# A layer with routed experts: filled TensorE waits, an earlier weight load, and shared work on the last routed rows

## The chip, the core and the metric

The kernel runs on one core of a Trainium2 chip. The core has five engines with a queue each: TensorE (PE, matrix products), VectorE (DVE), ScalarE (ACT), GpSimd (POOL) and SyncE (SP), which here only asks for transfers. 16 DMA engines carry the transfers. The metric is the device time of one execution in microseconds, as the median of the runs.

## The reference

One layer is computed for 128 prompt tokens and 512 sample tokens, five tiles of 128 rows, with a width of 1024. After norm, retention and differential attention, three projections lead to the residual `x1`. Then comes the part that matters here:

```python
h2 = rmsnorm(x, n2) * (1.0 + sc2) + sh2
x = x + g2 * hier_moe(h2, ...)          # and a last rmsnorm

# hier_moe: 4 groups of 8 experts, best group, best 2 experts in it
p_grp = softmax(hf @ rgw + rgb)
p_top, g_idx = top_k(p_grp, 1)
e_logits = (hf @ rew + reb).reshape(-1, 4, 8)     # those of the group
e_top, e_idx = top_k(softmax(e_logits), 2)
w = p_top * e_top / sum(e_top)
a = silu(hf @ wg[e]) * (hf @ wu[e])               # 256 wide
y = (a * w) @ wd[e]
```

Each of the 32 experts has 1 MB each of gate, up and down weights in fp32. All are read.

## The kernel before, in words

Every engine has its own program, written out by hand; semaphores tie them together. A list `plan`, which all engines walk, sets the order up to the last projection `wo1`; what follows it is written out one after the other for each engine.

**Rows and logits.** The tiles go in the order `ORDER = (4, 0, 1, 2, 3)`; tile 4 is the prompt. For a sample tile, VectorE multiplies `x1` by a scale row (`scaled_input`, plan item `M`), GpSimd forms the root of the mean square (`inverse_root`), and VectorE multiplies by the root and adds a shift row (`router_input`, plan item `N`): that is the tile `h2[t]`. It is stored to DRAM (`h2_dram`): the three middle tiles by SP (`row_store`, semaphore `st_h2_mid`), the last, tile 3, by ACT (`st_h2_ends`). TensorE forms the logits from `x1` without waiting for the root, 36 a token; VectorE scales them afterwards by the root, five small instructions, one for each tile, once the last root and the last rows are there.

**Routing.** VectorE picks group and experts in some 25 small instructions. TensorE counts ranks (L1328 to L1335, semaphore `pe_rank`), VectorE turns them into places, and TensorE's `places` (L1342) builds tables of which token stands in which place of an expert's block of 64: first rows (`idx_ready`), then choices, then weights.

**Experts.** Experts are worked in 16 pairs. For each pair GpSimd asks for an indirect transfer that gathers 128 token rows into `xg` (L2476, semaphores `ld_xg`), TensorE transposes them (`gathered`, L1359), ACT copies them out of PSUM, and TensorE multiplies with gate and up weights (L1366, in the first pair L1373 in two halves, semaphores `pe_gate0` and `pe_gu`), then with down weights (L1386, `pe_dn`). VectorE gates the rows, and GpSimd asks for the scattering transfer. At the end the rows of both experts are added and normalised.

**Weights.** SP asks for all weights, in the order of its program. There are six buffers for gate and up weights and six for down weights, three pairs' worth. Those of pairs 0 to 2 are asked for around `wo1` and behind it; those of pair 3 and later only when TensorE has finished with the buffer (`pe_gate0`, `pe_gu`, `pe_dn`). Between the two stands this stretch of SP's program (L925 to L936):

```python
load_gate_or_up(1, 3, 3); load_gate_up(2, 2)
for x in ld_xg: sp.wait_ge(x, 16)        # both gathers have landed
sp.wait_ge(x1_ready, 2 * NT); sp.wait_ge(st_h2_mid, 16 * 3)
load_down(4, 4)
sp.wait_ge(h2_ready, PT)
load_gate_or_up(1, 4, 4)
...                                      # two modulation rows, 0.5 MB each
```

`load_down(e, slot)` asks for an expert's down weights, `load_gate_or_up(g, e, slot)` for the gate (g = 0) or up (g = 1) weights. An instruction of SP that waits holds all behind it.

Of the kernel before, what the change touches and what calls it, by code (L numbers as in the profile page):

```python
# [27 lines left out]
ALU = mybir.AluOpType  # L28
# [3 lines left out]
P = 128  # L32
D = 1024
KC = D // P
HK = KC // 2
NT = 5
# [76 lines left out]
def build(nc, a, o, coff, roff, nconst, nroute):  # L113
    ctx = ExitStack()
    with ctx:  # L115
        sem_names = {}

        def sem(name):
            s = ctx.enter_context(nc.semaphore(name))
            sem_names[name] = s  # L120
            return s
# [529 lines left out]
        scale_made = sem("scale_made")  # L651
        prompt_scaled = sem("prompt_scaled")
# [35 lines left out]
        def _(sp):  # L688
# [149 lines left out]
            def load_down(e, slot):  # L838
                sp.dma_start(w_dn[slot], a["moe_w_down"][0, e].rearrange("(p k) n -> p k n", p=P)).then_inc(ld_dn[slot], 16)
# [86 lines left out]
            for x in ld_xg:  # L926
                sp.wait_ge(x, 16)
            sp.wait_ge(x1_ready, 2 * NT)
            sp.wait_ge(st_h2_mid, 16 * 3)
            load_down(4, 4)  # L930
            sp.wait_ge(h2_ready, PT)
            load_gate_or_up(1, 4, 4)
# [65 lines left out]
        def _(pe):  # L998
# [324 lines left out]

            pe.wait_ge(route_a, 1)
# [21 lines left out]
            halves = lambda v: v.rearrange("p (n i) -> p i n", i=2)  # L1346
            pe.wait_ge(route_a, 3)
# [3 lines left out]
            places(B(6), hot_rank, lambda x, i: halves(hot_row[:, x, 2, :])[:, i, :], PAIRS)  # L1351
            pe.wait_ge(route_d, 6)
# [68 lines left out]

            pe.wait_ge(idx_ready, 1)
            pe.wait_ge(ld_xg[0], 16)
            gathered(0).then_inc(pe_xt, 1)
            for p in range(PAIRS - 1):
                pair(p, p % 2, 2 * (p % 3), p // 2, p // 3, first=(p == 0))
# [64 lines left out]
        def _(act):  # L1491
# [236 lines left out]
            act.wait_ge(h2_ready, PT)  # L1728
            act.dma_start(h2_dram[3 * P:PT * P, :], h2[3]).then_inc(st_h2_ends, 16)
# [74 lines left out]
        def _(dve):  # L1804
            chain = [0]

            def link(ins):
                chain[0] += 1
                ins.then_inc(dve_chain, 1)
                dve.wait_ge(dve_chain, chain[0])  # L1810
# [226 lines left out]
            def router_input(t):  # L2037

                q = place_of[t]
                if q == 0:  # L2040
                    dve.wait_ge(ld_route, 16 * 6)
                    dve.wait_ge(ld_row2, 16 * 4)
                    for i in (1, 0):
                        dve.scalar_tensor_tensor(out=scale2[i], in0=scale2[i], scalar=1.0, in1=n2_row,
                                                 op0=ALU.add, op1=ALU.mult).then_inc(scale_made, 1)
                    dve.wait_ge(scale_made, 2)
                    return
                dve.wait_ge(roots, q + 1)
                dve.scalar_tensor_tensor(out=h2[t], in0=h2[t], scalar=rstd[:, t:t + 1], in1=shift2[0],
                                         op0=ALU.mult, op1=ALU.add).then_inc(h2_ready, 1)  # L2050
                if q < PT:
                    return

                dve.wait_ge(pe_logits, NT)
                for u in ORDER:
                    ins = dve.scalar_tensor_tensor(out=logits[:, u, :], in0=logit_out(u), scalar=rstd[:, u:u + 1],
                                                   in1=logit_bias[:, 1 if u == PT else 0, :], op0=ALU.mult, op1=ALU.add)
                link(ins)

            def scaled_input(t):  # L2060

                dve.wait_ge(x1_ready, x1_done[t])
                if t == 3:
                    dve.wait_ge(st_h2_ends, 16)
                link(dve.tensor_tensor(h2[t], x1[:, t, :], scale2[0], ALU.mult))
# [326 lines left out]
        def _(pool):  # L2392
# [74 lines left out]

            pool.wait_ge(idx_ready, 1)
# [16 lines left out]
            rows_in(1)  # L2485
            pool.wait_ge(idx_ready, 2)
# [56 lines left out]
```

## Time and profile before

| | us |
|---|---|
| median of 3 runs (lowest to highest) | 1154.61 (1154.06 to 1155.63) |
| the profiled execution | 1152.95 |
| its span | 1151.1 |

| engine | busy us | share of the span |
|---|---|---|
| TensorE | 1063.4 | 92% |
| VectorE | 580.1 | 50% |
| ScalarE | 404.4 | 35% |
| GpSimd | 101.2 | 9% |

The busy shares are means over stages with different limits. The page also cuts the span into 40 equal slices and gives for each the busy tenths, the granted clock of TensorE (9 is 90% or more of 2.4 GHz), the busy share of the DMA engines and the gigabytes a second they moved. The stretch of this change, from about 870 us, lies in slices 31 and 32. Matrix products overlap in TensorE's pipeline, so the time of a group is read from the start of its first to the end of its last, as the timeline gives it. The trace has two rows for each fp32 product.

### The profile page before, as it was taken

Reading aid. Unit: us, or ns where it says so; the run is one execution under the profiler, and the core shown is the slowest. Engines: PE = TensorE matmul, PEld = TensorE weight load, DVE = VectorE, ACT = ScalarE, POOL = GpSimd, SP = SyncE. Lnnn points to the kernel's source line nnn. Section 1 sums busy time; section 2 is a strip of 40 time slices with the busy share of each in tenths; the row PEclk is TensorE's granted clock in tenths of the full one; section 3 lists DMA queues with packets and bytes.
Section 4 is the critical chain, followed back from the end, with each engine's and each line's share of the span. In section 5 each row is a group of like instructions: output and inputs, shape, how many; then the busy total and the mean of one; then the engine's idle time right before and its main releaser. Section 6 shows DMA issues by size and latency. Waiting matters only on the chain. (4 is left out here: it accounts for less than half of the span.)

```text
span 1151.1 us, 13900 instructions
## 1 busy us (share of the span) xinstructions
PE 1063.4 (92%) x5491; PEld 770.7 (67%) x5491; DVE 580.1 (50%) x884; ACT 404.4 (35%) x795; POOL 101.2 (9%) x108
## 2 busy tenths in 40 slices
PE   3999999999999999999999999999995999878875
PEld 2688768888887777777886777788884433323332
DVE  4488715756545454452446666655648422212127
ACT  5352222222245565562227766441332111101104
POOL 1000011221000000000000101000021021111002
PEclk9999999999999999999999999999996999999998
DMA  8856743221532212314222221583627999999986
GB/s 300 264 185 229 244 178 109 93 65 56 163 102 84 91 56 64 120 56 137 74 83 64 62 65 48 192 341 132 256 86 316 409 420 420 420 420 420 420 360 258
DMA packets 71409, 226.16 MB, mean 196 GB/s; under 512 B 9389, under 2 KB 19942, under 8 KB 56882
## 3 DMA queue, kind: packets, MB, share of 16 engines
q1 hardware_dynamic: 64098, 209.40, 49.0%
q0 software_dynamic: 4464, 10.12, 2.3%
q10 hardware_dynamic: 2784, 5.77, 1.5%
q8 instruction: 44, 0.72, 0.2%
q14 instruction: 19, 0.16, 0.0%
HBM read 205.68 MB, written 25.72 MB: 201 GB/s over the span
## 5 line engine op out<-in xcount | busy, mean ns | idle before, releaser
L1127 PE MATMUL ps<-w_high,h_high 128*128 128x512 f32 x600 | 239.8, 400 | 0.5 <-ACT o_whole L1567 0.4
L1127 PE MATMUL ps<-w_high,h_low 128*128 128x512 f32 x600 | 234.2, 390 | 0.0
L1127 PE MATMUL ps<-w_low,h_high 128*128 128x512 f32 x600 | 233.6, 389 | 0.0
L1872 DVE TENSOR_TENSOR w_low<-w_loaded,w_high 128x2048 fp32r<-128x2048 f32 x44 | 101.3, 2303 | 109.7 <-ACT w_high L1520 109.7
L1127 PEld LDWEIGHTS ps<-w_high,h_high 128*128 128x128 f32 x600 | 112.9, 188 | 27.5 <-issue 4.2
L1127 PEld LDWEIGHTS ps<-w_high,h_low 128*128 128x128 f32 x600 | 112.6, 188 | 24.3
L1127 PEld LDWEIGHTS ps<-w_low,h_high 128*128 128x128 f32 x600 | 112.8, 188 | 22.2
L1366 PE MATMUL ps<-arena 128*64 128x512 f32 x448 | 103.4, 616 | 14.1 <-issue 14.0
L1520 ACT CAST w_high<-w_loaded 128x2048 fp32r<-128x2048 f32 x44 | 84.0, 1909 | 63.3 <-DMA w_loaded<-in_w_in 41.6
L1366 PEld LDWEIGHTS ps<-arena 128*64 128x64 f32 x448 | 35.2, 142 | 80.9 <-issue 80.9
L1628 ACT COPY arena<-ps 128x512 f32<-128x512 f32 x55 | 32.3, 588 | 153.2 <-PE ps L1127 152.7
L2173 DVE TENSOR_REDUCE neg_mx<-ps 128x1 f32<-128x768 f32 (+1 forms) x80 | 62.1, 818 | 43.0 <-PE ps L1287 43.0
L1747 ACT ACTIVATE arena<-ps 128x256 f32<-128x256 f32 x16 | 6.2, 384 | 188.4 <-PE ps L1366 168.6
L1705 ACT ACTIVATE arena<-ps,neg_mx 128x768 f32<-128x768 f32 (+1 forms) x80 | 63.2, 800 | 13.5 <-DVE neg_mx L2173 13.3
L1386 PE MATMUL ps<-arena 128*64 128x512 f32 x256 | 58.5, 599 | 8.1 <-ACT arena L1751 8.1
L2305 DVE SCALAR_TENSOR_TENSOR arena<-arena,ps 128x256 f32<-128x256 f32 x16 | 6.7, 422 | 114.2 <-ACT arena L1747 114.2
L1287 PE MATMUL ps<-arena 64*128 64x256 f32 (+2 forms) x288 | 53.9, 488 | 0.4 <-ACT arena L1705 0.4
L2320 DVE TENSOR_TENSOR arena<-ps,arena 128x1024 f32<-128x1024 f32 x16 | 19.6, 1225 | 56.7 <-PE ps L1386 31.5
L1320 PE MATMUL ps<-arena 128*128 128x128 f32 x384 | 48.0, 275 | 0.0
L1320 PEld LDWEIGHTS ps<-arena 128*128 128x128 f32 x384 | 46.3, 192 | 1.0
L1927 DVE SCALAR_TENSOR_TENSOR arena<-arena 128x2048 f32<-128x2048 f32 x20 | 45.9, 2350 | 0.5 <-DMA arena<-in_w_ada 0.5
L1386 PEld LDWEIGHTS ps<-arena 128*64 128x64 f32 x256 | 17.0, 136 | 39.4 <-issue 27.4
(303 smaller groups left out, 1641.0 us busy)
## 6 DMA issues: line engine op xcount, KB each, us to landing
arena<-in_moe_w_gate SPq DMA_DIRECT2D x32, 1024.0 KB, 23.1
arena<-in_moe_w_up SPq DMA_DIRECT2D x32, 1024.0 KB, 25.6
arena<-in_moe_w_down SPq DMA_DIRECT2D x32, 1024.0 KB, 26.5
w_loaded<-in_w_in SPq DMA_DIRECT2D x27, 1024.0 KB, 6.0
arena<-in_w_ada SPq DMA_DIRECT2D x24, 1024.0 KB, 6.6
w_loaded<-in_w_in ACTq DMA_DIRECT2D x5, 1024.0 KB, 5.3
y_rows<-arena SPq DMA_DIRECT2D x10, 512.0 KB, 7.0
gates<-arena SPq DMA_DIRECT2D x20, 256.0 KB, 2.0
```

Of the source, the lines that this page charges most:

```text
L1127: mm = pe.matmul(out, x[:, t, kk * P:(kk + 1) * P], w[w_buf(i)][:, k, :], start=(begins and k == 0 and j == 0), stop=(k == HK - 1 and j == ...
L1287: mm = pe.matmul(score[c][:, lo:hi], qT[h % 2][r, t * P:(t + 1) * P], keys, start=True, stop=True, skip_group_check=True)
L1320: mm = pe.matmul(pv_out, mixedT[s % 2][:, k * P:(k + 1) * P], v, start=(k == 0), stop=(k == 5))
L1366: mm = pe.matmul(B(bank_at)[BLK * i:BLK * (i + 1), :].rearrange("p (g f) -> p g f", g=2), xgT[slot][:, k, BLK * i:BLK * (i + 1)], w_gu[e0 ...
L1386: mm = pe.matmul(B(5 + n)[BLK * i:BLK * (i + 1), :], act_aT[slot][:, k, BLK * i:BLK * (i + 1)], w_dn[e0 + i][:, k, n * N512:(n + 1) * N512 ...
L1520: act.copy(w_hi[w_buf(i)][:], w_raw[w_buf(i)]).then_inc(w_rounded, 1)
L1628: free(act.copy(dst[:, t, c0:c0 + N512], src), n)
L1705: act.activation(probs[:, c, 0:n], score[c][:, 0:n], ACT.Exp, bias=neg_mx[:, s % 2, c:c + 1], scale=-1.0, accum_out=den[:, s % 2, c:c + 1] ...
L1872: dve.tensor_tensor(w_lo[b][:], w_raw[b], w_hi[b][:].bitcast(F32), ALU.subtract).then_inc(w_split, 1)
L1927: ins = dve.scalar_tensor_tensor(out=total, in0=ada_place[i % 2], scalar=ccol[:, k, s:s + 1], in1=total, op0=ALU.mult, op1=ALU.add)
L2173: dve.tensor_reduce(neg_mx[:, s % 2, c:c + 1], score[c][:, 0:n], AXX, ALU.min).then_inc(max_ready, 1)
L2320: return dve.tensor_tensor(y_out[:, par, :], psf[:, 5 * N512:7 * N512], g2_of, ALU.mult)
```

## The change

- SP no longer waits for the gathers (`ld_xg`) ahead of `load_down(4, 4)`. Behind it, two waits are new: for `rows_asked`, which GpSimd raises when it has issued the first two gathers, and for `last_half`.
- TensorE gets `keep_going(n, b)`: n products of the identity with itself (128x128x128, fp32) into PSUM bank b, whose results nobody reads. 26 stand ahead of the rank products, 7 ahead of the first table, 9 ahead of the table of weights, 7 ahead of the first gathered transposes, and 6 behind them, ahead of the first pair.
- VectorE scales the logits of the first four tiles ahead of the wait for the last root, and the last tile's logits after it.
- The last tile's rows `h2[3]`: VectorE makes columns 0 to 511; GpSimd makes columns 512 to 1023, in a multiply and an add. ACT's row store and SP's second load wait for both (`last_half`).

The names `last_scaled`, `last_half` and `rows_asked` are new names for semaphores that an earlier stage has left at 4, so the waits are for 5.

```diff
@@ SP, behind wo1
             load_gate_or_up(1, 3, 3)
             load_gate_up(2, 2)
-            for x in ld_xg:
-                sp.wait_ge(x, 16)
             sp.wait_ge(x1_ready, 2 * NT)
             sp.wait_ge(st_h2_mid, 16 * 3)
             load_down(4, 4)
+            sp.wait_ge(rows_asked, chunks_before + 1)
             sp.wait_ge(h2_ready, PT)
+            sp.wait_ge(last_half, chunks_before + 1)
             load_gate_or_up(1, 4, 4)
@@ TensorE
+            def keep_going(n, b=0):
+                for _ in range(n):
+                    pe.matmul(B(b)[:, 0:P], C("ident"), C("ident"), start=True, stop=True)
+            wait_freed(pe, where[("mm", "wo1", ORDER[3])])
+            keep_going(26)
             pe.wait_ge(route_a, 1)
             pe.wait_ge(route_d, 2)
...
+            keep_going(7)
             pe.wait_ge(route_a, 3)
             pe.wait_ge(route_d, 4)
             places(B(5), ...)
             pe.wait_ge(route_d, 5)
             places(B(6), ...)
+            keep_going(9)
             pe.wait_ge(route_d, 6)
             places(B(7), ...)
...
+            keep_going(7)
             pe.wait_ge(idx_ready, 1)
             pe.wait_ge(ld_xg[0], 16)
             gathered(0).then_inc(pe_xt, 1)
+            keep_going(6, 2)
@@ ACT
             act.wait_ge(h2_ready, PT)
+            act.wait_ge(last_half, chunks_before + 1)
             act.dma_start(h2_dram[3 * P:PT * P, :], h2[3]).then_inc(st_h2_ends, 16)
@@ VectorE, router_input and scaled_input
+                if q == PT:
+                    dve.wait_ge(pe_logits, PT)
+                    for u in ORDER[:PT]:
+                        scaled_logits(u)
                 dve.wait_ge(roots, q + 1)
-                dve.scalar_tensor_tensor(out=h2[t], in0=h2[t], ..., in1=shift2[0], ...)
+                cols_of = slice(0, N512 if q == PT else D)
+                dve.scalar_tensor_tensor(out=h2[t][:, cols_of], in0=h2[t][:, cols_of], ..., in1=shift2[0][:, cols_of], ...)
-                dve.wait_ge(pe_logits, NT)
-                for u in ORDER:
-                    ins = dve.scalar_tensor_tensor(out=logits[:, u, :], in0=logit_out(u), ...)
-                link(ins)
+                if q == PT:
+                    dve.wait_ge(pe_logits, NT)
+                    link(scaled_logits(t))
...
+                if place_of[t] == PT:
+                    ins.then_inc(last_scaled, 1)
+                    dve.wait_ge(last_scaled, chunks_before + 1)
@@ GpSimd
+            t = ORDER[PT]
+            pool.wait_ge(last_scaled, chunks_before + 1)
+            pool.wait_ge(roots, NT)
+            link(pool.tensor_scalar(h2[t][:, N512:D], h2[t][:, N512:D], rstd[:, t:t + 1], None, ALU.mult))
+            pool.tensor_tensor(h2[t][:, N512:D], h2[t][:, N512:D], shift2[0][:, N512:D], ALU.add).then_inc(last_half, 1)
...
             rows_in(0)
             rows_in(1)
+            pool.sem_inc(rows_asked, 1)
```

On TensorE, from the rank products (L1328 before, L1337 now) to the first pair's gate and up products (L1373 before, L1384 now), the program held these rows:

```order
L1328 MATMUL ps<-arena 128x160
L1331 MATMUL ps<-arena 128x32 x10
L1335 MATMUL ps<-arena 128x32 x5
L1342 MATMUL ps<-arena 64x32 x20
L1342 MATMUL ps<-arena 64x16 x40
L1359 MATMUL ps<-const,arena 128x128 x8
L1373 MATMUL ps<-arena 64x256 x32
```

It holds these now (L1329 are the identity products, L1351 the tables, L1370 the gathered transposes):

```order
L1329 MATMUL ps<-const 128x128 x26
L1337 MATMUL ps<-arena 128x160
L1340 MATMUL ps<-arena 128x32 x10
L1344 MATMUL ps<-arena 128x32 x5
L1329 MATMUL ps<-const 128x128 x7
L1351 MATMUL ps<-arena 64x32 x20
L1351 MATMUL ps<-arena 64x16 x20
L1329 MATMUL ps<-const 128x128 x9
L1351 MATMUL ps<-arena 64x16 x20
L1329 MATMUL ps<-const 128x128 x7
L1370 MATMUL ps<-const,arena 128x128 x8
L1329 MATMUL ps<-const 128x128 x6
```

55 products were added in five places, and nothing else moved on this engine.

On VectorE, from the last tile's multiply by the scale row (L2065 before) to the first instructions of the routing (L2202), with what each waits for:

```order
L2065 TENSOR_TENSOR arena<-arena 128x1024 [waits st_h2_ends,x1_ready]
L2049 SCALAR_TENSOR_TENSOR arena<-arena,rstd 128x1024 [waits roots,dve_chain]
L2056 SCALAR_TENSOR_TENSOR const<-ps,rstd,const 128x36 [waits pe_logits]
L2056 SCALAR_TENSOR_TENSOR const<-ps,rstd,const 128x36 x4
L2202 TENSOR_REDUCE arena<-const 128x5 [waits dve_chain]
```

And now (L2083 is the multiply, L2063 the logits; `chunk_rows` is the semaphore behind `last_scaled`):

```order
L2083 TENSOR_TENSOR arena<-arena 128x1024 [waits st_h2_ends,x1_ready]
L2063 SCALAR_TENSOR_TENSOR const<-ps,rstd,const 128x36 [waits pe_logits,chunk_rows]
L2063 SCALAR_TENSOR_TENSOR const<-ps,rstd,const 128x36 x3
L2072 SCALAR_TENSOR_TENSOR arena<-arena,rstd 128x512 [waits roots]
L2063 SCALAR_TENSOR_TENSOR const<-ps,rstd,const 128x36 [waits pe_logits]
L2225 TENSOR_REDUCE arena<-const 128x5 [waits dve_chain]
```

Four of the five logit instructions moved ahead of the wait for the root, and the row instruction covers 512 columns.

On SP, the loads behind `wo1`, before:

```order
L828 DMA arena<-in_moe_w_up 128x2048 [waits pe_dense]
L828 DMA arena<-in_moe_w_gate 128x2048
L828 DMA arena<-in_moe_w_up 128x2048
L839 DMA arena<-in_moe_w_down 128x2048 [waits x1_ready,st_h2_mid,ld_xg1,ld_xg0]
L828 DMA arena<-in_moe_w_up 128x2048 [waits h2_ready]
L936 DMA arena<-mod_rows_dram 128x1024 [waits st_h2_ends,pe_logits]
```

And now (`pe_select` is the semaphore behind `rows_asked`, `chunk_cols` the one behind `last_half`):

```order
L830 DMA arena<-in_moe_w_up 128x2048 [waits pe_dense]
L830 DMA arena<-in_moe_w_gate 128x2048
L830 DMA arena<-in_moe_w_up 128x2048
L841 DMA arena<-in_moe_w_down 128x2048 [waits st_h2_mid,x1_ready]
L830 DMA arena<-in_moe_w_up 128x2048 [waits chunk_cols,h2_ready,pe_select]
L938 DMA arena<-mod_rows_dram 128x1024 [waits st_h2_ends,pe_logits]
```

The order of the transfers is the same; what the down load and the up load wait for has changed.

## Rows read from the trace of the kernel before

**Rows 1.** Stretches: us, busy PE, PEld, DVE, ACT, POOL, PE clock, DMA share, GB/s.

```profile
870.00:880.00 10.00, 1.46 (x23) 1.26 (x22) 9.01 (x32) 0.88 (x3) 0.00 (x0) 0.67 1.02 422
880.00:890.00 10.00, 5.47 (x88) 4.96 (x88) 8.47 (x35) 1.07 (x2) 2.69 (x3) 0.50 0.42 135
884.00:888.00 4.00, 3.40 (x46) 3.36 (x47) 3.59 (x17) 0.00 (x0) 1.12 (x2) 0.50 0.60 168
890.00:900.00 10.00, 9.92 (x104) 7.12 (x104) 4.72 (x14) 0.38 (x1) 0.60 (x1) 0.81 1.00 374
950.00:1100.00 150.00, 124.74 (x576) 47.51 (x574) 34.14 (x40) 18.32 (x40) 19.26 (x19) 0.97 1.02 420
```

**Rows 2.** Timeline of TensorE: start us, us, line, operation, [idle before and releaser].

```profile
691.44 1.50 PE L1320 MATMUL ps<-arena 128*128 128x128 f32 x12
...
878.04 0.29 PE L1328 MATMUL ps<-arena 128*128 128x160 bf16 x1 [7.28 <-DVE arena L2226]
...
880.72 1.24 PE L1342 MATMUL ps<-arena 128*64 128x32 bf16 x40 [1.98 <-DVE arena L2235]
884.60 2.32 PE L1342 MATMUL ps<-arena 128*64 128x16 f32 x40 [2.64 <-DVE arena L2254]
886.89 1.94 PE L1359 MATMUL ps<-const,arena 128*128 128x128 f32 x8
890.08 8.94 PE L1373 MATMUL ps<-arena 128*64 128x256 f32 x64 [1.25 <-ACT arena L1742]
...
1031.25 10.00 PE L1366 MATMUL ps<-arena 128*64 128x512 f32 x32 [2.98 <-issue]
...
1097.18 7.09 PE L1366 MATMUL ps<-arena 128*64 128x512 f32 x32 [2.96 <-issue]
```

**Rows 3.** Timeline of SP's queue: start us, us, line, transfer.

```profile
867.90 0.33 SPq L836 DMA_DIRECT2D h_rows<-arena  x1
...
869.29 0.46 SPq L828 DMA_DIRECT2D arena<-in_moe_w_up  x1
888.62 0.33 SPq L839 DMA_DIRECT2D arena<-in_moe_w_down  x1
...
895.60 0.81 SPq L828 DMA_DIRECT2D arena<-in_moe_w_gate  x2
...
913.25 0.33 SPq L828 DMA_DIRECT2D arena<-in_moe_w_gate  x1
```

**Rows 4.** Issues at 867.9, 888.6, 871.1, 882.8, 913.2: KB, us to landing.

```profile
h_rows<-arena SPq DMA_DIRECT2D x1, 512.0 KB, 6.8
...
arena<-in_moe_w_down SPq DMA_DIRECT2D x1, 1024.0 KB, 4.7
...
h_rows<-arena ACTq DMA_DIRECT2D x1, 512.0 KB, 8.3
...
arena<-h_rows,row_idx POOLq DMA_INDIRECT x1, 3.9
...
arena<-in_moe_w_gate SPq DMA_DIRECT2D x1, 1024.0 KB, 7.3
```

**Rows 5.** Timeline of GpSimd.

```profile
852.55 2.38 POOL L2466 TENSOR_TENSOR arena<-arena 128x1024 f32<-128x1024 f32 x1
...
882.82 1.27 POOL L2476 DMA_INDIRECT arena<-h_rows,row_idx  x1 [13.15 <-DVE to_idx L2243]
884.40 1.03 POOL L2476 DMA_INDIRECT arena<-h_rows,row_idx  x1 [0.31 <-issue]
```

**Rows 6.** Timeline of VectorE, then line L2012: duration ns min/median/max.

```profile
854.17 1.31 DVE L2012 TENSOR_TENSOR arena<-arena 128x512 f32<-128x512 f32 x1
...
869.78 1.28 DVE L2049 SCALAR_TENSOR_TENSOR arena<-arena,rstd 128x1024 f32<-128x1024 f32 x1 [0.77 <-POOL rstd L2457]
870.98 0.90 DVE L2056 SCALAR_TENSOR_TENSOR const<-ps,rstd,const 128x36 f32<-128x36 f32 x5
...
L2012 DVE TENSOR_TENSOR arena<-arena x10: 691/692/1307, 817.6 to 866.0; 128x512 f32<-128x512 f32 x10
```

More of the change, by code:

```diff
@@ L651, in build @@
         scale_made = sem("scale_made")
+        last_scaled, last_half, rows_asked = chunk_rows, chunk_cols, pe_select
+        chunks_before = 4
         prompt_scaled = sem("prompt_scaled")
@@ L2047, in router_input, with scaled_logits @@
                     return
+                def scaled_logits(u):
+                    return dve.scalar_tensor_tensor(out=logits[:, u, :], in0=logit_out(u), scalar=rstd[:, u:u + 1],
+                                                    in1=logit_bias[:, 1 if u == PT else 0, :], op0=ALU.mult, op1=ALU.add)
+                if q == PT:
+                    dve.wait_ge(pe_logits, PT)
+                    for u in ORDER[:PT]:
+                        scaled_logits(u)
                 dve.wait_ge(roots, q + 1)
-                dve.scalar_tensor_tensor(out=h2[t], in0=h2[t], scalar=rstd[:, t:t + 1], in1=shift2[0],
+                cols_of = slice(0, N512 if q == PT else D)
+                dve.scalar_tensor_tensor(out=h2[t][:, cols_of], in0=h2[t][:, cols_of], scalar=rstd[:, t:t + 1], in1=shift2[0][:, cols_of],
                                          op0=ALU.mult, op1=ALU.add).then_inc(h2_ready, 1)
-                if q < PT:
-                    return
-                dve.wait_ge(pe_logits, NT)
-                for u in ORDER:
-                    ins = dve.scalar_tensor_tensor(out=logits[:, u, :], in0=logit_out(u), scalar=rstd[:, u:u + 1],
-                                                   in1=logit_bias[:, 1 if u == PT else 0, :], op0=ALU.mult, op1=ALU.add)
-                link(ins)
+                if q == PT:
+                    dve.wait_ge(pe_logits, NT)
+                    link(scaled_logits(t))
             def scaled_input(t):
@@ L2064, in scaled_input @@
                     dve.wait_ge(st_h2_ends, 16)
-                link(dve.tensor_tensor(h2[t], x1[:, t, :], scale2[0], ALU.mult))
+                ins = dve.tensor_tensor(h2[t], x1[:, t, :], scale2[0], ALU.mult)
+                if place_of[t] == PT:
+                    ins.then_inc(last_scaled, 1)
+                    dve.wait_ge(last_scaled, chunks_before + 1)
+                else:
+                    link(ins)
             def router_weights(n):
```

## The prediction, as written before the result

> **What bounds the kernel now.** I read the page's slices first, then stretches of 10 us from 870 us on, then the queue of SP, then TensorE's timeline over the same 30 us, and last the landings of single transfers. Two things are to be seen.
>
> The first is that the expert stage is bound by its transfers. From 950 to 1100 us the DMA engines are busy throughout (share 1.02, 420 GB/s) while TensorE works 124.7 of 150 us [rows 1]. Two pairs of experts late in it start 1097.18 - 1031.25 = 65.9 us apart, over four pairs, 16.5 us for each [rows 2]; TensorE's own work of one is 124.7 x 16.5 / 150 = 13.7 us. So a microsecond that TensorE saves in the middle of this stage is worth nothing by itself. What counts is when the stream of weights starts to run without a hole, because each later landing is that much earlier.
>
> The second is the hole. From 870 to 880 us the DMA share is 1.02, from 880 to 890 it is 0.42, from 890 on 1.00 [rows 1]: 5.8 us of transfer time are lost between the last product of `wo1` and the first expert. SP's queue shows why. It asks for an expert's up weights at 869.29 and then for nothing until 888.62 [rows 3]; the next load stands there behind a wait for both gathers. Meanwhile TensorE waits 7.28 us for the routing and falls to 1.2 GHz (granted clock 0.67 from 870 to 880, 0.50 from 880 to 890 [rows 1]); the first expert pair's gate and up products take 8.94 us [rows 2].
>
> **The held block.** `load_down(4, 4)` (1 MB) no longer waits for the two gathers, only for the row stores of the middle tiles. The last of these is asked for at 867.9 and lands 6.8 us later [rows 3, 4], at 874.7, so this load joins the queue behind three others and runs right after them. At 420 GB/s (1 MB is 1.05 million bytes) it fills 2.5 us of the hole, to about 883.8: the stream before it runs out at 881.3, as of the 4.2 us busy after 880 the gathers take 2.4 (0.60 of 884 to 888) and the request at 888.62 some 0.5 [rows 1, 3]. The up half of expert 4 is now asked for once GpSimd has issued both gathers, not once they have landed: 884.40 + 1.03 + a little, 885.8, not behind the request at 888.62 [rows 3, 5]. From the 888.62 request to a full stream took some 1.3 us (I read it from the share, 0.42 to 890, 1.00 after), so it moves data from about 887.2. The residue of the hole here is 887.2 - 883.8 - 2.4 = 1.0, call it 1.2 us with the gathers slowed.
>
> Behind that stand 1 MB of up weights, 1 MB of modulation rows and the third gather, 0.5 MB: 6.2 us, so the queue is dry at 893.6. The next request waits for TensorE (`pe_gate0`), at 895.60 before [rows 3]. How early TensorE gets there is therefore the second term.
>
> **The routing chain on VectorE.** Scaling five tiles' logits took 0.90 us after the last rows' 1.28 us [rows 6]. Four of the five move into the wait of 0.77 us, and the row operation is halved to 0.69 us (the duration of 512 columns in the row of L2012 [rows 6]). The last logits leave TensorE at 878.04 - 7.28 = 870.76 [rows 2], so the last scaling ends near 871.05 in place of 871.88: 0.8 us earlier.
>
> GpSimd's half speaks against it. It is a multiply and an add over 512 columns. The nearest GpSimd row is the add over 1024 columns, 2.38 us [rows 5], so 1.2 us each; a multiply with one tensor input may take half. The trace shows what happens beside such an add: L2012, two tiles in SBUF, began at 854.17 while GpSimd's add ran from 852.55 to 854.93, and took 1.31 us where its median is 0.69 [rows 5, 6]. So one overlap cost 0.6 us. Two may come here, on the row operation and on the small two-tile operations of the routing: bounds 0 and 2.4 - 0.7 = 1.7 us. I take 1.1, near two of the seen ones, and the chain to TensorE comes out 0.3 us LATER (bounds 0.8 earlier and 0.9 later).
>
> The Trainium skill, "SBUF — State Buffer", section "Who interferes with whom", says the same by a stronger rule: a VectorE instruction with two SBUF inputs and a GpSimd instruction that reads SBUF exclude each other for the whole instruction. By that rule both of GpSimd's halves hold up VectorE in full and the chain is near the late bound; without it the chain would be 0.8 us earlier and the sum below 1.1 us better. Our one overlap agrees with the rule.
>
> The last tile's row store leaves ACT after GpSimd's add, near 872.6, not 871.09, and with the 8.3 us it took it lands at 880.9 [rows 4]. The gathers are asked for at 882.82 [rows 5], so 1.9 us of cover are left; if the released load pushes the store back by its own 2.5 us, 0.6 us show.
>
> **The identity products.** Six products of 128x128x128 in fp32 took 1.50 us at full clock, 0.25 us each [rows 2]. 26 take 6.5 us in a wait of 7.28; seven take 1.75 us in the wait of 1.98; nine take 2.25 us in a wait of 2.64 that also grows as the placing products run at full clock. All of these are covered. The seven before the first gathered transposes are not: before, the transposes followed the placing products without a gap at 886.89 [rows 2]. Now the placing products (2.32 us at 1.2 GHz, some 1.2 at 2.4) end at 884.6 + 0.3 + 1.2 = 886.1, and the seven end at 887.8. The gather lands 3.9 us after its request [rows 4], 882.82 + 0.3 + 3.9 = 887.0, or 888 if the released load shares the engines: about even. So transposes start 0.9 us later than before. Then the clock pays: eight transposes took 1.94 us at 1.2 GHz, and I take 1.2 at full clock, ACT's copy as before but six products (1.5 us) in a wait of 1.25, then the first half of 8.94 against 7.1 us. Gate products end at 887.8 + 1.2 + 1.5 + 3.5 = 894.0, so the request at 895.60 moves to 894.0: 1.6 us earlier (0.5 to 2.7).
>
> **The sum.** The queue is dry at 893.6, the gate weights flow from 894.0 + 1.3 = 895.3: a second residue of 1.7 us. The hole shrinks from 5.8 to 1.2 + 1.7 = 2.9 us, a gain of 2.9. Can TensorE's later releases hold it? They come 1.6 us earlier too. The fifth pair's first gate load, asked for at 913.25, landed 7.3 us after its request, where a load into an idle queue took 4.7 [rows 3, 4]: 2.6 us of backlog, so up to 1.6 + 2.6 = 4.2 us of gain can pass. It does. From there all landings shift by about 3.0 us, the last pair's too, and what follows it is unchanged work. The profiled execution took 1152.95 us and would take 1149.95; the median of the runs is 1.66 us above it, so I forecast 1154.61 - 3.0 = 1151.6 us.
>
> **Rivals.**
> - All of the hole closes. The GpSimd half doesn't disturb VectorE (chain 0.8 us earlier), the gathers land at once and `pe_gate0` comes 2.7 us earlier, so the second residue is nearly gone: a gain of 5, 1149.6 us. Against it: the overlap row, and a row store that must land first. Chance 0.15.
> - Given back to TensorE's releases: the gap is closed by the released load, but the queue runs dry again at `pe_gate0`, which comes only 0.5 us earlier or no earlier, as the seven products and the late store eat what the clock gives. The second residue is 2.8 us or more, the gain 1.5: 1153.1 us, no change to be told. For it: everything on that path is even to within half a microsecond. Chance 0.18.
> - The clock falls in a later wait. One pair's products took 10.00 us at 1.2 GHz after a wait of 2.98 us, another's 7.09 after 2.96 [rows 2]. The waits shift, and if the one before the next to last pair is hit, the stream's gain goes back in 2.9 us: 1154.5 us. It can hit either kernel in any run. Chance 0.10.
> - Slower: the fillers run at 1.2 GHz. If the 26 products don't hold the clock they take 13 us in a wait of 7.28, the rank products come 5.7 us late, VectorE waits for them (`pe_rank`), and so do both gathers and `pe_gate0`: 895.60 + 5.7 - 1.6, near 899.7, data from 901.0 where before they flowed from about 898 (backlog of the 890 burst). 3 us slower, 1157.6. The point from which it decides is 0.28 us for a product, 7.28 / 26. Against it: the granted clock, 0.67 over 870 to 880, was 1.00 for the first 3.4 us of it and 0.50 after, so it fell 2.6 us into the idle wait and not before [rows 1]. Chance 0.10, with a gather held behind the released load for far longer than 2.5 us in the same class.
> - That the change doesn't do what it says I count at nothing: the orders show each part in its place.
>
> **Numbers.** The forecast has 0.47 (its own range 1150.4 to 1152.3), the rivals 0.15, 0.18, 0.10 and 0.10. A measurement of this kernel can tell 0.2%, 2.3 us. Faster by that is the forecast and the first rival, 0.62; within it the second and third, 0.28; slower 0.10. The range leaves out part of the outermost: 1149.0 to 1154.9 us.
>
> **What would show it.** Right: DMA share near 0.75 from 880 to 890 us; SP's down load at about 875 and its up load at about 886; granted clock 1.00 through the routing; transposes near 887.8; `pe_gate0`'s loads near 894; the second hole at 894. Wrong: the fillers at over 0.28 us each, a row store landing after 882, small VectorE operations all at their old durations beside GpSimd's (then the first rival), or late pairs not shifted although the hole is filled.

## The result, and the profile after

Against the kernel before on the same chip, the median over 20 runs each went from 1155.81 to 1158.99 us: a ratio of 1.003, 95% interval 1.002 to 1.004. The change made the kernel slower by some 3 us. The forecast was 1151.6.

Two executions of the changed kernel were profiled: the first took 1155.3 us, the shortest of its 20, the second (`e5_again` below) 1159.87, near the median. Over the profiles the end of the last logits product lies anywhere from 869.86 to 873.17 us, though TensorE's work ahead of it is unchanged: 870.77 before, 872.04 in the first, 873.03 in the second. So moments are compared below as us from that end.

The stretches of the first, with the same columns as [rows 1]:

```profile
870.00:880.00 10.00, 8.32 (x86) 8.16 (x85) 8.88 (x29) 1.47 (x6) 4.21 (x4) 1.00 1.02 421
880.00:890.00 10.00, 7.97 (x134) 7.37 (x130) 8.79 (x34) 0.15 (x2) 2.27 (x2) 1.00 0.95 365
890.00:900.00 10.00, 9.20 (x84) 6.85 (x86) 5.18 (x17) 1.07 (x2) 1.16 (x1) 1.00 0.66 231
950.00:1100.00 150.00, 126.57 (x578) 47.66 (x576) 34.12 (x40) 18.30 (x40) 20.25 (x20) 0.95 1.02 420
```

The reader is to see that the hole of 880 to 890 us is filled (share 0.42 before, 0.95 now), and that another stands in the next ten (1.00 before, 0.66 now). Over the twenty the engines were busy for 14.2 us before and 16.1 now; part of this is only that the logits ended 1.27 us later, and a count from their end follows below. TensorE's clock is granted in full in the first three of these stretches (0.67, 0.50 and 0.81 before).

TensorE's timeline (start, us, line, operation, idle before), to be held against [rows 2]:

```profile
871.87 6.05 PE L1329 MATMUL ps<-const 128*128 128x128 f32 x52
879.60 0.23 PE L1337 MATMUL ps<-arena 128*128 128x160 bf16 x1 [1.68 <-DVE arena L2249]
...
880.05 1.81 PE L1329 MATMUL ps<-const 128*128 128x128 f32 x14
...
886.91 1.83 PE L1329 MATMUL ps<-const 128*128 128x128 f32 x14
890.80 1.13 PE L1370 MATMUL ps<-const,arena 128*128 128x128 f32 x8 [2.06 <-DMA arena<-h_rows,row_idx]
...
893.20 7.13 PE L1384 MATMUL ps<-arena 128*64 128x256 f32 x64
```

The identity products run at 0.233 us each and hold the clock. But the transposes now wait 2.06 us for the gathered rows. Before they began 16.1 us after the logits and waited for no gather; now 18.8.

SP's queue answers to [rows 3]:

```profile
870.66 0.53 SPq L830 DMA_DIRECT2D arena<-in_moe_w_up  x1
875.72 0.33 SPq L841 DMA_DIRECT2D arena<-in_moe_w_down  x1
884.32 0.33 SPq L830 DMA_DIRECT2D arena<-in_moe_w_up  x1
884.74 2.21 SPq L938 DMA_DIRECT2D arena<-mod_rows_dram  x2
896.91 1.33 SPq L830 DMA_DIRECT2D arena<-in_moe_w_gate  x2
```

GpSimd's timeline, to be held against [rows 5]:

```profile
871.12 2.08 POOL L2494 TENSOR_SCALAR arena<-arena,rstd 128x512 f32<-128x512 f32 x1 [0.18 <-POOL rstd L2480]
873.29 1.26 POOL L2495 TENSOR_TENSOR arena<-arena 128x512 f32<-128x512 f32 x1
884.06 1.28 POOL L2505 DMA_INDIRECT arena<-h_rows,row_idx  x1 [9.51 <-DVE to_idx L2266]
885.65 0.99 POOL L2505 DMA_INDIRECT arena<-h_rows,row_idx  x1 [0.31 <-issue]
```

The rows to read together are SP's 884.32 and GpSimd's 884.06 and 885.65. SP asks for the up weights 0.26 us after the first gather's instruction has begun and 1.33 us before the second's, and for the modulation rows 0.42 us later. The increment of `rows_asked` stands behind both gathers in GpSimd's program, and the page's waits (us in total, times, longest) name it as what released SP:

```profile
SPq L830 <- POOLq L2515: 8.2, 1, 8.2
```

So 2 MB are asked for between and beside the two gathers of 0.5 MB each. The landings (transfer, KB where given, us from request), which were 3.9 and 4.2 us for the two gathers before:

```profile
arena<-h_rows,row_idx POOLq DMA_INDIRECT x1, 6.6
...
arena<-h_rows,row_idx POOLq DMA_INDIRECT x1, 7.9
...
h_rows<-arena ACTq DMA_DIRECT2D x1, 512.0 KB, 8.0
```

The second execution is worse in each step. Its stretches, its TensorE (again with the idle time before) and SP:

```profile
882.00:885.00 3.00, 3.00 (x50) 2.75 (x49) 1.82 (x6) 0.00 (x0) 0.00 (x0) 0.50 1.05 440
890.00:900.00 10.00, 8.18 (x76) 6.64 (x74) 6.90 (x22) 1.07 (x2) 0.99 (x1) 1.00 0.60 220
```

```profile
880.59 0.23 PE L1337 MATMUL ps<-arena 128*128 128x160 bf16 x1 [1.68 <-DVE arena L2249]
...
881.04 2.68 PE L1329 MATMUL ps<-const 128*128 128x128 f32 x14
883.65 1.24 PE L1351 MATMUL ps<-arena 128*64 128x32 bf16 x40
884.81 4.06 PE L1329 MATMUL ps<-const 128*128 128x128 f32 x18
...
893.73 1.13 PE L1370 MATMUL ps<-const,arena 128*128 128x128 f32 x8 [1.82 <-DMA arena<-h_rows,row_idx]
```

```profile
886.01 0.33 SPq L830 DMA_DIRECT2D arena<-in_moe_w_up  x1
...
899.85 0.33 SPq L830 DMA_DIRECT2D arena<-in_moe_w_gate  x1
```

Here the clock fell although the 26 products had run: seven of the next took 2.68 us in place of 1.81, the first table stood behind them without idle time, and the gather was asked for 12.7 us after the logits. It landed 7.8 us later, the transposes began at 20.7, the gate load came at 26.8.

The stream over the first 70 us from the last logits (columns of [rows 1]) carries it to the end; before, and the two executions of the change:

```profile
870.77:940.77 70.00, 53.25 (x390) 27.29 (x390) 34.65 (x99) 7.84 (x19) 9.40 (x9) 0.85 0.93 374
```

```profile
872.04:942.04 70.00, 61.93 (x500) 36.10 (x499) 34.76 (x94) 7.79 (x19) 11.97 (x11) 1.00 0.95 376
```

```profile
873.03:943.03 70.00, 63.12 (x490) 38.13 (x491) 34.16 (x92) 7.28 (x17) 11.81 (x11) 0.95 0.91 357
```

At 420 GB/s, (374 - 357) x 70 / 420 = 2.8 us of transfer are missing in the second, and its next-to-last pair of experts starts 3.7 us later than before. In the first nothing is missing (-0.3 us), and that pair starts 0.3 us earlier; its own 2.35 us over the profiled time before are made up mostly by the 1.27 of the late start and by a fall of the clock in the last down product, 5.35 us where before it took 3.65. Before and after:

```profile
1120.11 3.65 PE L1386 MATMUL ps<-arena 128*64 128x512 f32 x16 [0.46 <-ACT arena L1751]
```

```profile
1121.10 5.35 PE L1397 MATMUL ps<-arena 128*64 128x512 f32 x16 [0.46 <-ACT arena L1765]
```

### The profile page after: what moved, and what is told of

Its sections match the earlier page's. It is cut to its first block, busy times and chain, and to the rows that moved or that the text cites. A ratio compares the mean times of both kernels' runs of the same rounds, so it can differ in the third digit from the quotient of the medians.

```text
span 1153.5 us, 14125 instructions
## 1 busy us (share of the span) xinstructions
PE 1075.5 (93%) x5601; PEld 780.4 (68%) x5601; DVE 580.5 (50%) x884; ACT 404.0 (35%) x795; POOL 104.7 (9%) x110
## 4 chain that ended last, share of the span: by engine, by line
PE 74%; DVE 8%; ACT 8%; issue 5%; DMA 4%; SPq 1%; ACTq 0%; DVEq 0%
PE ps L1129 41%; PE ps L1377 9%; PE ps L1397 5%; PE ps L1289 3%; DMA arena<-in_w_ada 3%; PE ps L1322 2%; ACT arena L1718 2%; PE ps L1306 2%; DVE arena L1941 2%; PE ps L1083 2%; PE ps L1160 2%; ACT w_high L1533 1%; PE ps L1370 1%; PE ps L1384 1%; PE ps L1174 1%
## 5 line engine op out<-in xcount | busy, mean ns | idle before, releaser
L1377 PE MATMUL ps<-arena 128*64 128x512 f32 x448 | 104.9, 623 | 12.3 <-issue 12.3
L1397 PE MATMUL ps<-arena 128*64 128x512 f32 x256 | 60.2, 613 | 8.2 <-ACT arena L1765 8.2
## 6 DMA issues: line engine op xcount, KB each, us to landing
arena<-in_moe_w_gate SPq DMA_DIRECT2D x32, 1024.0 KB, 22.6
arena<-in_moe_w_up SPq DMA_DIRECT2D x32, 1024.0 KB, 24.8
arena<-in_moe_w_down SPq DMA_DIRECT2D x32, 1024.0 KB, 26.1
```

The costliest lines, as they stand in the source:

```text
L1377: mm = pe.matmul(B(bank_at)[BLK * i:BLK * (i + 1), :].rearrange("p (g f) -> p g f", g=2), xgT[slot][:, k, BLK * i:BLK * (i + 1)], w_gu[e0 ...
L1397: mm = pe.matmul(B(5 + n)[BLK * i:BLK * (i + 1), :], act_aT[slot][:, k, BLK * i:BLK * (i + 1)], w_dn[e0 + i][:, k, n * N512:(n + 1) * N512 ...
```

## The experiments

All moments in the table are us after the end of the last logits product; "pair" is the start of the next-to-last pair's products, GB/s the mean over those 70 us. There is one profile of each kernel, two of the change. A ratio is to the kernel before on the same chip, which took 1155.9 to 1156.5 us on the chips of the experiments; intervals of 0.1 to 0.15% either way mean that differences under some 0.2% are not told apart.

| kernel | gathers land after | transposes | gate load | pair | GB/s | median us | ratio (95%) |
|---|---|---|---|---|---|---|---|
| before | 3.9 / 4.2 | 16.1 | 24.8 | 226.4 | 374 | 1155.8 | 1 |
| after | 6.6 / 7.9 | 18.8 | 24.9 | 226.1 | 376 | 1159.0 | 1.003 (1.002 to 1.004) |
| e5_again | 7.8 / 8.4 | 20.7 | 26.8 | 230.1 | 357 | 1159.8 | 1.003 (1.002 to 1.005) |
| e1_no_half | 7.8 / 8.9 | 19.0 | 26.7 | 229.1 | 360 | 1158.6 | 1.003 (1.002 to 1.004) |
| e2_no_fill | 7.6 / 8.1 | 20.1 | 29.3 | 232.2 | 343 | 1160.6 | 1.004 (1.003 to 1.005) |
| e3_held | 3.8 / 4.1 | 16.5 | 22.6 | 226.4 | 373 | 1156.7 | 1.000 (0.999 to 1.002) |
| e4_up_after_rows | 4.0 / 4.3 | 17.7 | 23.7 | 225.4 | 378 | 1154.6 | 0.999 (0.998 to 1.000) |
| e6_release_only | 3.9 / 4.4 | 16.1 | 24.7 | 225.4 | 377 | 1156.8 | 1.001 (0.999 to 1.002) |
| e8_rows_later | 6.5 / 5.8 | 19.1 | 25.2 | 228.5 | 371 | 1157.7 | 1.001 (1.000 to 1.003) |
| e7_first_rows | 4.2 / 4.2 | 15.6 | 21.6 | 224.0 | 390 | 1153.9 | 0.998 (0.997 to 0.9995) |
| e9_first_rows_no_fill | 4.6 / 4.1 | 16.1 | 25.6 | 226.8 | 370 | 1156.6 | 1.000 (0.998 to 1.001) |
| e10_logits_only | 3.9 / 4.3 | 15.4 | 24.1 | 225.8 | 377 | 1153.7 | 0.998 (0.9965 to 0.9995) |
| e11_second_rows | 4.2 / 4.1 | 15.6 | 21.6 | 224.0 | 390 | 1153.6 | 0.998 (0.996 to 0.999) |
| e12_half_held | 3.9 / 4.3 | 16.4 | 26.1 | 228.6 | 364 | 1157.6 | 1.001 (0.999 to 1.002) |

**One part undone.** `e1_no_half`: VectorE makes all of the last rows.

```diff
-            pool.tensor_tensor(h2[t][:, N512:D], h2[t][:, N512:D], shift2[0][:, N512:D], ALU.add).then_inc(last_half, 1)
...
-            act.wait_ge(last_half, chunks_before + 1)
...
-            sp.wait_ge(last_half, chunks_before + 1)
...
-                cols_of = slice(0, N512 if q == PT else D)
+                cols_of = slice(0, D)
```

> The changed kernel with VectorE making all 1024 columns of the last rows again, GpSimd none. Theory 1 (the gathers land late because 2 MB of other requests go with them): the gathers still take over 6 us to land, TensorE's first gate products end at most 1 us earlier counted from the last logits, and the time stays within 1.5 us of the changed kernel (about 1158). Theory 2 (GpSimd's half holds up VectorE and the row store): the 1.28 us instruction of VectorE's routing is back at 0.18, the row store goes out 2.3 us earlier, and the time falls by 2 to 3 us, to the kernel before.

1.003, as the change: the half is not the cause by itself. The gather was asked for 1.0 us earlier after the logits (11.0 against 12.0), and this gain went into a landing of 7.8 us. TensorE waited 3.29 us for the rows, and the clock fell: the eight transposes took 1.94 us, and the gate load came at 26.7.

`e2_no_fill`: without the 55 identity products.

```diff
-            wait_freed(pe, where[("mm", "wo1", ORDER[3])])
-            keep_going(26)
...
-            keep_going(7)
...
-            keep_going(9)
...
-            keep_going(7)
...
-            keep_going(6, 2)
```

> The changed kernel without the 55 identity products. Theory 1: the gathers land late all the same, and on top the first pair's products run at 1.2 GHz (8.9 in place of 7.1 us), so the first gate products end 1 to 2 us later than in the changed kernel: 1160 to 1161. Theory 3 (the fillers cost more than they bring, in the path or in the clock of later waits): 1156 or less.

The slowest median of all, though its interval (1.003 to 1.005) overlaps that of the change. So the identity products don't make the loss; that they cover some of it fits the gate load at 29.3, 2.5 to 4.4 us later than in the change, and is not clear of the noise in the time. Its transposes wait longest for the gather:

```profile
890.57 1.94 PE L1366 MATMUL ps<-const,arena 128*128 128x128 f32 x8 [3.66 <-DMA arena<-h_rows,row_idx]
```

`e3_held`: SP waits for both gathers ahead of the down load again, all else as in the change.

```diff
+            for x in ld_xg:
+                sp.wait_ge(x, 16)
             sp.wait_ge(x1_ready, 2 * NT)
             sp.wait_ge(st_h2_mid, 16 * 3)
             load_down(4, 4)
-            sp.wait_ge(rows_asked, chunks_before + 1)
```

> The changed kernel with SP waiting for both gathers ahead of the down load, as before. Theory 1: the gathers land in about 4 us, the first gate products end 2 to 3 us earlier than in the changed kernel counted from the last logits, while the hole of the transfers is back; the time is that of the kernel before or up to 1.5 us better (1154.5 to 1156). Theories 2 and 3: no change against the changed kernel beyond 1 us (1158 to 1159).

The gathers land in 3.8 and 4.1 us again and the loss is gone (1.000); the median, 1156.7, is still 0.7 us above the range expected. The loss comes with the new order of SP. A second thing is to be seen here: the gate load comes 2.2 us earlier than before (22.6 against 24.8), and the late pair starts at the same 226.4. The hole ahead of the down load is back, and behind it the transfers still had a backlog when the gate load was asked for, so asking earlier brought nothing.

`e4_up_after_rows`: the down load stays released, the wait for `rows_asked` becomes one for both landings.

```diff
             load_down(4, 4)
-            sp.wait_ge(rows_asked, chunks_before + 1)
+            for x in ld_xg:
+                sp.wait_ge(x, 16)
```

> The changed kernel, with the down load released but the up load and the two modulation rows behind a wait for both gathers' landing. Theory 1: the gathers land in 4 to 5 us, the first gate products end about 2 us earlier, and the share of the DMA engines from 880 to 900 is better than in either kernel: 1153 to 1155. Theories 2 and 3: 1158 to 1159.

```profile
arena<-h_rows,row_idx POOLq DMA_INDIRECT x1, 4.0
```

0.999 (0.998 to 1.000), 0.4% better than the change, although in its profile the clock fell behind the rank products. Of what the change let go early, it is what stands behind `rows_asked` that brings the loss. The share from 880 to 900 us was not the best of the three, as I had expected: 15.9 us busy against 14.2 before and 16.1 in the change.

**The change once more and the rest of SP's order.** `e5_again` is the change unaltered; its profile stands above, and its gather (7.8 us) and gate load (26.8) came as Theory 1 said.

> The changed kernel once more, for a second profile. Its first profiled execution took 1155.3 us, the shortest of 20 (median 1159.0), with the first gather landing 6.6 us after its request. Theory 1 says that the loss is set by how the gather fares among the other requests: in an execution near the median the gather lands 7.5 to 8.5 us after its request and the first gate load is asked for about 1.5 us later than in the first profile, counted from the last logits (26 to 27 us). Theory 4 (the loss is in the late stage, by the clock or by the transfers there): gather and gate load as in the first profile (6.6 and 24.9 us).

`e6_release_only`: the kernel before with the down load released and nothing else.

```diff
-            for x in ld_xg:
-                sp.wait_ge(x, 16)
...
             load_down(4, 4)
+            for x in ld_xg:
+                sp.wait_ge(x, 16)
```

> The kernel before with one thing moved: the down load of expert 4 ahead of the wait for the gathers, all else behind it as before. Theory 1: its transfer runs out before the gathers ask, so it costs them at most 1 us (landing in 4 to 5 us), and a small gain or none: 1154.5 to 1156. Rival (any load that joins the queue ahead of the gathers delays them): landing above 5.5 us, 1157 or more.

Gathers at 3.9 and 4.4 us: the transfers run at a full share until about 1 us after the first gather's request, and that tail costs it nothing to be seen. The pair starts 1.0 us earlier, too little for the median to tell (1.001, 0.999 to 1.002); no gain shows, and 1156.8 is above the range I expected.

`e8_rows_later`: the change, with only the modulation rows (1 MB) behind both landings; the up weights (1 MB) still go with the gathers.

```diff
             sp.wait_ge(st_h2_ends, 16 * 2)
+            for x in ld_xg:
+                sp.wait_ge(x, 16)
```

> The changed kernel with only the two modulation rows (1 MB) behind the landing of both gathers; the up load (1 MB) still goes when GpSimd has asked for them. Theory 1: a loss between the kernel with both behind it (1154.6) and the changed one (1158.9), the gather landing in 5 to 6 us. If the modulation rows are harmless, it equals the changed kernel, 1158 to 1159; if they do all the harm, 1154 to 1155.

In between in the time (1.001), though its interval overlaps those on both sides. In the landings the second gather is in between (5.8 us), and the first, at 6.5, is as late as in the first profile of the change (6.6) and above the 5 to 6 us expected: most of its delay comes with the up weights alone. Over all profiles the landings are 3.8 to 4.6 us where nothing is asked for until the first gather is in, 6.5 and 5.8 with 1 MB, 6.6 to 8.9 with 2 MB.

**Without the half, SP held for one landing.** `e7_first_rows` is `e1_no_half` with the wait for `rows_asked` turned into one for the first gather's landing.

```diff
-            sp.wait_ge(rows_asked, chunks_before + 1)
+            sp.wait_ge(ld_xg[0], 16)
```

> The changed kernel with VectorE making all of the last rows, and with the up load of expert 4 and the modulation rows behind the landing of the first gather alone. Theory 1: the gather is asked for 1 us earlier and lands in 4 to 5 us, the first gate load is asked for at 21.5 to 23 us after the last logits (24.8 before), the hole of the transfers is shorter than before: 1152 to 1154, better than the kernel before. Rival: the second gather, now with 2 MB beside it, comes too late for the second pair: 1155 or more.

Faster than before, 0.9983 (0.9971 to 0.9995). Its stretches:

```profile
880.00:890.00 10.00, 9.22 (x142) 8.82 (x141) 8.80 (x36) 0.91 (x2) 2.44 (x3) 1.00 0.87 314
890.00:900.00 10.00, 9.89 (x118) 7.18 (x116) 6.63 (x22) 0.84 (x3) 0.82 (x1) 1.00 0.99 386
```

Later loads, yet more bytes over the twenty (18.6 us busy in place of 16.1): 0.87 in place of 0.95 in the first ten, 0.99 in place of 0.66 in the next, since TensorE frees its buffers earlier. Its up load is asked for 15.3 us after the logits and the gate load at 21.6, where the change has 12.3 and 24.9. The second gather, still under way when the 2 MB are asked for, lands in 4.2 us all the same.

`e9_first_rows_no_fill` is `e7_first_rows` without identity products (diff of `e2_no_fill`).

> The kernel of e7 (up load and modulation rows behind the first gather, VectorE makes all last rows) without the 55 identity products. If the fillers bring what the clock gives in the first pair, the first gate load is asked for 2.3 to 3 us later than in e7 (24 to 24.5 us after the last logits in place of 21.6), the transfers run dry ahead of it, and the time is 1 to 2 us above e7's: 1155 to 1156. Rival (transfers set the pace anyway, the fillers are worth nothing): the same as e7, 1153.9.

The gate load comes 4.0 us later (25.6; 24 to 24.5 expected), and the transfers all but stop ahead of it (shares of 0.05 and 0.03 from 24 to 26 us after the logits). The median is 1156.55 against 1153.92, and 1153.62 in `e11_second_rows` on the same chip: the products are worth some 0.2% once the gather is in time.

`e11_second_rows` is `e7_first_rows` with `sp.wait_ge(ld_xg[1], 16)` ahead of the modulation rows.

> The kernel of e7 with the modulation rows behind the second gather, so that only 1 MB goes beside it. Theory 1: the second gather was not in anyone's way in e7 (landed in 4.2 us), so nothing is gained: within 0.7 us of e7's 1153.9. Rival: the modulation rows still cost the first pair something, 1152.5 to 1153.2.

0.998 (0.996 to 0.999), not to be told from `e7_first_rows`.

**The logits and the half by themselves.** `e10_logits_only`: the kernel before with four tiles' logits scaled ahead of the last root, and nothing else of the change.

```diff
+                if q == PT:
+                    dve.wait_ge(pe_logits, PT)
+                    for u in ORDER[:PT]:
+                        scaled_logits(u)
                 dve.wait_ge(roots, q + 1)
```

> The kernel before with one thing changed: four tiles' logits scaled ahead of the wait for the last root (VectorE then makes all 1024 columns). The gather is asked for 1.0 us earlier (11.0 in place of 12.0 us after the last logits), everything behind it too, the hole of the transfers starts at the same time and ends 1 us earlier: about 1 us better than the kernel before. Rival (the hole's end is set elsewhere): no change.

`e12_half_held`: the same with the last rows shared with GpSimd.

```diff
+            link(pool.tensor_scalar(h2[t][:, N512:D], h2[t][:, N512:D], rstd[:, t:t + 1], None, ALU.mult))
+            pool.tensor_tensor(h2[t][:, N512:D], h2[t][:, N512:D], shift2[0][:, N512:D], ALU.add).then_inc(last_half, 1)
```

> The kernel of e10 (four tiles' logits ahead, nothing else) with the last rows shared with GpSimd as in the changed kernel: the price of that share alone. By the profiles of the changed kernel VectorE loses 1.1 us in one small routing instruction beside GpSimd's add, which is what the early logits bring: the gather is asked for at 12.0 us after the last logits, not 11.0, and the time is that of the kernel before, 1 to 2.5 us above e10. Rival (the row store or VectorE's delay is hidden): the same as e10.

0.998 (0.9965 to 0.9995) without the half, 1.001 (0.999 to 1.002) with it: the early logits alone gain 0.2%, and the half takes 3 to 4 us of median back (1153.66 to 1157.55, on two chips; 1 to 2.5 were expected). `e10_logits_only` also bears on `e9_first_rows_no_fill`: on the same chip the latter, which adds SP's new order with the loads held for the first gather, took 2.9 us more. Without the identity products the earlier loads only moved the hole to the gate load: there it ran dry at 24 to 26 us, where `e10_logits_only` kept a share of 0.96 and more. (Its full clock also came back later, 24.6 us after the logits against 22.3.)

What the half does to VectorE is seen in the same small operation in both; first without, then with it:

```profile
872.29 0.18 DVE L2228 TENSOR_TENSOR arena<-arena 128x20 f32<-128x20 f32 x1
```

```profile
873.91 0.18 DVE L2228 TENSOR_TENSOR arena<-arena 128x20 f32<-128x20 f32 x1
...
874.33 1.28 DVE L2230 TENSOR_TENSOR arena<-arena 128x20 f32<-128x20 f32 x1
```

And on GpSimd beside the second of these:

```profile
872.15 2.08 POOL L2489 TENSOR_SCALAR arena<-arena,rstd 128x512 f32<-128x512 f32 x1 [0.18 <-POOL rstd L2475]
874.32 1.26 POOL L2490 TENSOR_TENSOR arena<-arena 128x512 f32<-128x512 f32 x1
```

The counterpart of the 0.18 us at 872.29 is the 1.28 at 874.33, which stands for as long as GpSimd's add. The gather was asked for 12.3 us after the logits in place of 11.4, and the gate load 26.1 in place of 24.1. The first microsecond of this is accounted for by the blocked operation. The other one lies in the first pair's products, without and with the half:

```profile
889.55 8.89 PE L1380 MATMUL ps<-arena 128*64 128x256 f32 x64 [1.25 <-ACT arena L1749]
```

```profile
892.66 9.88 PE L1381 MATMUL ps<-arena 128*64 128x256 f32 x64 [1.25 <-ACT arena L1751]
```

They began at 1.2 GHz in both, and the full clock came back 22.3 us after the logits in one and 25.2 in the other. Why it came back later there stays open, with one profile of each; so of the 3 to 4 us, 1 us is shown to be the half's.

## Why the prediction was wrong, point by point

- **The failed step** is in "The held block": "The up half of expert 4 is now asked for once GpSimd has issued both gathers ... 885.8", and with it, in "The identity products", "The gather lands 3.9 us after its request ... or 888 if the released load shares the engines". The request came 0.26 us after the first gather's instruction had begun and before the second's, and the landings were 6.6 to 8.4 us. I looked for the disturber in the down load, which has all but run out by then (`e6_release_only`: 3.9 and 4.4). The up weights and modulation rows that stand right behind it I counted as bytes for the stream and not as traffic beside the gathers. `e4_up_after_rows` moves only these behind the landings and takes the loss away. The rival "Slower" (0.10) took in a gather held back "for far longer than 2.5 us", which is what came, but by the released load and not by those behind it.
- What followed was worked out in the right form with the wrong landing. Transposes 2.6 us later than before (4.6 in the second profile) where 0.9 was forecast; the gate load at the old place or 2.0 us later where 1.6 earlier was. The hole that the down load was to fill did close: the first residue, forecast at 1.2 us, was 0.5 (share 0.95 from 880 to 890 us). The stream then ran thin from 892 to 898 us (shares of 0.53, 0.63 and 0.27): 3.4 us lost from 890 to 900, the "second residue", which I had at 1.7 us. The second rival ("given back to TensorE's releases", 0.18) named this place but not a loss: it let `pe_gate0` come no later than before.
- **The stream sets the end**: borne out. Over the profiles, the bytes of the first 70 us give the shift of the next-to-last pair: -2.7 us worked out and -2.4 seen in `e7_first_rows`, 5.2 and 5.8 in `e2_no_fill`, 2.8 and 3.7 in `e5_again`. It holds within 0.9 us in all but `e8_rows_later` (0.5 and 2.1). From 224.0 (`e7_first_rows`) to 232.2 us (`e2_no_fill`) the medians rise from 1153.9 to 1160.6, with `e6_release_only` some 2 us above such a line and `e10_logits_only` as much below it; the change stands on it with its second profile and 3.4 us above it with its first.
- **GpSimd's half**: the size of the chain was right (a gather asked for 12.0 us after the logits, as before, 0.3 later forecast), its parts were not. The multiply took 2.08 us, not at most 1.2; it left VectorE's operations alone (0.18 us at 872.88 in the change), and the add blocked one of them in full.

```profile
871.02 0.74 DVE L2072 SCALAR_TENSOR_TENSOR arena<-arena,rstd 128x512 f32<-128x512 f32 x1
872.08 0.26 DVE L2063 SCALAR_TENSOR_TENSOR const<-ps,rstd,const 128x36 f32<-128x36 f32 x1 [0.31 <-PE ps L1198]
...
872.88 0.18 DVE L2233 TENSOR_TENSOR arena<-arena 128x20 f32<-128x20 f32 x1
...
873.30 1.28 DVE L2235 TENSOR_TENSOR arena<-arena 128x20 f32<-128x20 f32 x1
```

  The Trainium skill, "SBUF — State Buffer", section "Who interferes with whom", holds that a VectorE instruction with two SBUF inputs contends with a GpSimd instruction that reads SBUF, under an exclusive lock. The add's row agrees, the multiply's does not: the small operation at 872.88 has two such inputs and ran at its old length inside the multiply's 871.12 to 873.20. Whether the 2.08 us hold a wait of GpSimd for VectorE's row operation, which ran to 871.76, no run shows: the two overlap alike in every profile that has the half.

  The row store left ACT 2.3 us later than before, counted from the logits, and landed 8.0 us after, 1.4 us before the gather was asked for; it did not show.
- **The identity products**: right where they held the clock (26 in 6.05 us, transposes 1.13 us, first half pair 7.13). I had their failure as a rival only for the first 26. It came behind them: an idle wait of 1.68 us stood after the 26 in both executions, and in one of them the clock then fell. This put 0.7 us on the path, with the products themselves in the way of the first table. The half has a part in it: it makes this wait 1 us longer. With it the clock fell behind the rank products in three of five profiles (`e5_again`, `e4_up_after_rows`, `e8_rows_later`; not in the first of the change and in `e3_held`); without it the wait is 0.70 us, and it fell there in none of three (`e1_no_half`, `e7_first_rows`, `e11_second_rows`). With so few profiles this is a hint and no proof. One reading of [rows 2] was loose: the pair of 10.00 us had a granted clock of 0.50 only from 1031 to 1037 us and 1.00 from 1039 on; its price of 2.9 us stands.
- **The early logits**: the chain was to gain 0.8 us by them and the half's shorter row operation together. By themselves they bring 0.7 (`e10_logits_only`: rank products 6.6 us after the logits in place of 7.3), so the half gives VectorE 0.1 us and costs it 1.1. Of the three parts run alone (early logits, released down load, and the half on top of the early logits) they are the only one with a gain clear of the noise.

Left open: how much of the 3 us each cause has in a typical execution. Held loads give back 0.3 to 0.4% (`e3_held`, `e4_up_after_rows`), the half costs 0.3% where the gather is in time (`e12_half_held`) and nothing to be told where it is not (`e1_no_half`). That the two don't add up because both delay the same transposes is likely and was not tested.

## What to carry to other kernels

When a wait for landed data is relaxed to "has been asked for", look at everything queued behind it: here 2 MB of loads not needed yet brought the landing of the first rows, on which the whole chain waited, from 3.9 to 6.6 and 7.8 us, and holding them for one landing moved more bytes in the end (`e7_first_rows`). Where a stream is fed by releases from a compute engine, an earlier request and an earlier release pay only together: the request alone moved the hole to the next release (`e9_first_rows_no_fill`), and the release alone came while the stream still had a backlog (`e3_held`). Time the parts of a bundle alone: here the smallest edit, four instructions moved into a wait, was worth as much, within the noise, as any version with all the others mended.

## What the runs showed of the hardware

- An increment placed behind two indirect transfers in GpSimd's program let SP go 0.26 us after the first of them had begun and 1.33 us before the second, in the trace of the change; in the second profile (885.75 and 886.01) and in `e1_no_half`, `e2_no_fill` and `e8_rows_later` it was 0.26 us after as well. So it does not say that both gathers are under way.
- Gathers of 0.5 MB landed 3.8 to 4.6 us after their request where nothing was asked for until the first was in, 6.5 and 5.8 us with 1 MB of plain loads asked for right behind the first, 6.6 to 8.9 with 2 MB. A second gather that had 2 MB asked for beside it 2.6 us after its own request (`e7_first_rows`) still landed in 4.2. The Trainium skill, "DMA: Bandwidth & Descriptors", section "Queues, rings and completion order", says that each engine takes turns between the queues it has work for, a packet at a time; that fits a gather which is slowed by a load beside it, and no run here tells it from other ways of sharing.
- A GpSimd multiply by a per-partition factor over 512 columns took 2.08 us beside VectorE's row operation, and an add 1.26 (1.27 in two profiles). VectorE's small operations with two SBUF inputs kept their 0.17 to 0.18 us inside the multiply; the one that met the add took 1.28, about the add's whole length. It was so in all seven profiles with the half.
- The same program held TensorE's full clock through the routing in one execution; in another, behind a wait of 1.68 us and the rank products, the granted clock went to 0.50 (1.2 GHz).
